# Negating the filter taps on GpSimd, and building the first spectrum before the second filter's rows

## The reference

```python
def bidir_long_conv(u, h_fwd, h_bwd, bias):
    filt = concat([h_fwd, zeros(1), h_bwd[1:][::-1]])
    spec = rfft(u, 2n) * rfft(filt, 2n)
    return irfft(spec)[:n] + u * bias
def hyena(u, lp):
    x1, x2, v = split(short_conv(u), 3)
    filt = hyena_filters(n, lp)        # a small MLP with sines, times exp(-t * decay)
    z = v
    for o, g in enumerate((x1, x2)):
        z = g * bidir_long_conv(z, filt[:, o, 0], filt[:, o, 1], bias[o])
    return z
def trunk_layer(x, mod, lp):
    shift, scale, gate = split(mod, 3)      # mod = silu(c) @ ada_w + ada_b
    h = rmsnorm(x) * (1 + scale) + shift
```

## Time and profile before

| what | value |
|---|---|
| median of 3 runs | 2737.1 us (2736.19 to 2737.31) |
| the profiled execution | 2737.1 us, span 2734.9 us |
| TensorE busy | 2426.1 us, 89% of the span |
| VectorE busy | 1319.2 us, 48% |
| ScalarE busy | 943.0 us, 34% |
| GpSimd busy | 172.8 us, 6% |
| mean granted clock of TensorE | 0.942 |

### The profile page before, as it was taken

One profiled execution on the slowest core, in us unless ns is written; L12 is line 12 of the kernel. 1 busy time (PEld: TensorE's weight loads), 2 busy tenths in 40 slices (PEclk: granted clock), 3 DMA queues, 4 the chain that ended last, 5 costly groups with the idle time before them and its releaser, 6 DMA issues. The chain is left out here.

```text
span 2734.9 us, 33688 instructions
## 1 busy us (share of the span) xinstructions
PE 2426.1 (89%) x13152; PEld 1596.1 (58%) x13152; DVE 1319.2 (48%) x2658; ACT 943.0 (34%) x1886; POOL 172.8 (6%) x184
## 2 busy tenths in 40 slices
PE   3999999899898987879859999999988989888798
PEld 1765765674476756554327567557745667565543
DVE  3352664564364474661133426545553644746611
ACT  2242113541253364651022421135412533646510
POOL 0120000001000000001202200010010000000012
PEclk8999999999999998989969999999999989989799
DMA  6430100100100000102155101000001000001021
GB/s 216 165 140 26 50 16 1 48 1 13 58 7 9 3 1 2 63 1 91 60 178 213 61 26 50 16 21 29 1 13 64 1 9 3 1 2 63 1 93 61
DMA packets 72136, 128.42 MB, mean 47 GB/s; under 512 B 22915, under 2 KB 36099, under 8 KB 70341
## 3 DMA queue, kind: packets, MB, share of 16 engines
q1 hardware_dynamic: 71864, 121.52, 13.0%
q10 hardware_dynamic: 112, 4.72, 0.5%
HBM read 109.02 MB, written 21.92 MB: 48 GB/s over the span
## 5 line engine op out<-in xcount | busy, mean ns | idle before, releaser
L609 PE MATMUL psum<-arena 128*32 128x256 f32 (+8 forms) x8496 | 1743.0, 451 | 123.8 <-DMA arena<-in_hy_decay 46.9
L609 PEld LDWEIGHTS psum<-arena 128*32 128x32 f32 (+3 forms) x8496 | 1013.1, 161 | 780.7 <-issue 526.3
L613 PE MATMUL psum<-ident,arena 128*128 128x128 f32 (+1 forms) x2248 | 366.6, 291 | 76.2 <-ACT arena L1284 30.0
L1763 DVE TENSOR_REDUCE st<-psum 128x1 f32<-128x1152 f32 (+1 forms) x288 | 352.0, 1235 | 137.1 <-PE psum L609 135.5
L1469 DVE TENSOR_TENSOR arena<-arena 128x64 f32<-128x64 f32 (+10 forms) x686 | 304.5, 490 | 175.8 <-ACT arena L1420 57.5
L613 PEld LDWEIGHTS psum<-ident,arena 128*128 128x128 f32 (+1 forms) x2248 | 268.1, 146 | 178.6 <-issue 59.7
L1268 ACT ACTIVATE arena<-psum,st 128x1152 f32<-128x1152 f32 (+1 forms) x288 | 324.8, 1129 | 118.8 <-DVE st L1763 115.3
L609 PE MATMUL psum<-k_parts,q_parts 96*128 96x384 f32 (+2 forms) x1000 | 300.4, 391 | 34.4 <-ACT arena L1268 22.9
L1284 ACT COPY arena<-psum 128x512 f32<-128x512 f32 (+1 forms) x344 | 170.6, 505 | 230.3 <-PE psum L613 229.2
L1469 DVE TENSOR_TENSOR arena<-psum,arena 128x512 f32<-128x512 f32 (+2 forms) x136 | 75.1, 553 | 355.6 <-PE psum L609 308.2
L609 PEld LDWEIGHTS psum<-k_parts,q_parts 96*128 96x128 f32 (+1 forms) x1000 | 181.5, 205 | 53.3 <-ACT arena L1268 36.6
(11 more groups left out here) (125 smaller groups left out, 1170.1 us busy)
## 6 DMA issues: line engine op xcount, KB each, us to landing
arena<-in_ada_w SPq DMA_DIRECT2D x12, 2048.0 KB, 9.0
arena<-in_w_in SPq DMA_DIRECT2D x10, 2048.0 KB, 9.0
arena<-out_xs SPq DMA_DIRECT2D x36, 512.0 KB, 4.7
out_xs<-arena SPq DMA_DIRECT2D x18, 512.0 KB, 2.6
arena<-in_w_out SPq DMA_DIRECT2D x4, 2048.0 KB, 7.9
out_xs<-in_x ACTq DMA_DIRECT2D x1, 4608.0 KB, 17.3
spectrum_kept<-arena SPq DMA_DIRECT2D x2, 2304.0 KB, 8.4
arena<-spectrum_kept SPq DMA_DIRECT2D x2, 2304.0 KB, 8.8
```

Source lines behind the costliest of these rows:

```text
L609: return nc.tensor.matmul(out, lhsT, rhs, start=start, stop=stop)
L613: return nc.tensor.transpose(out, src, ident[0:n, 0:n])
L1763: nc.vector.tensor_reduce(st[:, 16 + x % 4:17 + x % 4], psum[:, 512 * b0:512 * (b0 + nk)].rearrange("p (c n) -> p c n", c=nk)[:, :, 0:w], ...
```

## The change

It has four parts.

1. The copy of the tokens is started by SP, behind the six constants, and SP waits for it at the head of each layer, before the first parameter load. Before, ACT started it, and SP waited for it later.
2. The negation of the filter rows moves from ACT's list to GpSimd's: nine instructions of 128x256 in front of each butterfly, so 36 in the run.
3. On DVE the filter rows of o = 0 and the bias of slice 3 come behind the whole first spectrum.
4. On SP the store of the first spectrum comes ahead of the six token loads.

The numbers of lines shift a little: L1469 becomes L1463, L1597 L1586, L1608 and L1610 L1597 and L1599, L2016 L2007, and the negation is L2048.

```diff
--- before.py
+++ after.py
@@ -431,6 +431,7 @@
             sp.dma_start(craw[:, :, 1:2], I["c_ctx"].rearrange("(o k p) -> p k o", p=P, o=1)).then_inc(S.raw("constants"), 16)
             sp.dma_start(halves[:, :], I["halves"]).then_inc(S.raw("constants"), 16)
             sp.dma_start(negt[:, :], I["negt"]).then_inc(S.raw("constants"), 16)
+            sp.dma_start(xs[0], I["x"]).then_inc(S.raw("x_copied"), 16)
             with sp.Fori(0, DEPTH) as l:
                 def lay(name):
                     return I[name][bass.ds(l, 1)]
@@ -455,6 +456,7 @@
                     load(W[:, SLOT[c], :, 0:n], src.rearrange("o (k p) n -> p (o k) n", p=P),
                          f"weights{SLOT[c]}_loaded", c)
 
+                sp.wait_ge(S.raw("x_copied"), 16)
                 load(at(F_FEAT, TOK, parts=33), I["feats"], "filter_params")
                 load(at(A_FW, 64, parts=33), lay("hy_fw1").rearrange("o k n -> (o k) n"), "filter_params")
                 load(at(A_FW + 64, 64, parts=64), lay("hy_fw2").rearrange("o k n -> (o k) n"), "filter_params")
@@ -482,18 +484,17 @@
                 chunk()
                 chunk()
 
+                sp.wait_ge(*S.at("butterfly_pool", ("F", 1)))
+                sp.wait_ge(*S.at("spectrum1_made"))
+                sp.dma_start(spectrum_kept, at(HS, 4608)).then_inc(*S.up("spectrum1_kept", None, 16))
+
                 def load_x(t):
                     load(at(XN[t % RING], D), xs[bass.ds(l, 1)][:, rows(t), :].rearrange("o p n -> (o p) n"),
                          f"x{t % RING}_loaded", t)
 
-                sp.wait_ge(S.raw("x_copied"), 16)
                 sp.wait_ge(*K.emptied(("f3", 0, NT)))
                 for t in range(RING):
                     load_x(t)
-                sp.wait_ge(*S.at("butterfly_pool", ("F", 1)))
-                sp.wait_ge(*S.at("spectrum1_made"))
-                sp.dma_start(spectrum_kept, at(HS, 4608)).then_inc(*S.up("spectrum1_kept", None, 16))
-
                 chunk()
                 chunk()
 
@@ -1103,7 +1104,6 @@
                 act.wait_ge(*S.now("scalar_step"))
 
             act.wait_ge(S.raw("constants"), 16 * N_CONST)
-            act.dma_start(xs[0], I["x"]).then_inc(S.raw("x_copied"), 16)
             nc.scalar.activation(csil[:, :, :], craw[:, :, :], ACT.Tanh, scale=0.5).then_inc(S.raw("silu_ready"), 1)
             act.wait_ge(S.raw("ones_set"), 1)
             with act.Fori(0, DEPTH) as l:
@@ -1125,12 +1125,6 @@
                                          accum_out=st[:, t:t + 1]).then_inc(*S.up("x_squares", t))
 
                 for o in (1, 0):
-                    for t in range(TT):
-                        act.wait_ge(*K.emptied(("f3", o, t)))
-                        if t in (0, NT):
-                            act.wait_ge(*S.at("lag0_cleared", (o, t)))
-                        last = nc.scalar.mul(at(EO, TT, 3, GW)[:, t, 2, :], at(EO, TT, 3, GW)[:, t, 1, :], -1.0)
-                    last.then_inc(*S.up("filter_negated", o))
                     if o == 0:
 
                         act.wait_ge(*S.at("butterfly_sums", ("F", 1)))
@@ -1557,8 +1551,7 @@
 
                 add_ada_bias(0)
                 eo = at(EO, TT, 3, GW)
-                def filter_rows(o):
-
+                for o in (1, 0):
                     for t in range(TT):
                         job = ("f3", o, t)
                         v.wait_ge(*K.full(job))
@@ -1573,15 +1566,11 @@
 
                             v.wait_ge(*K.emptied(job))
                             nc.vector.memset(eo[0:1, t, 1, :], 0.0).then_inc(*S.up("lag0_cleared", (o, t)))
-
-                filter_rows(1)
-                add_ada_bias(1)
-                add_ada_bias(2)
-                add_ada_bias(3)
-                filter_rows(0)
-                add_ada_bias(4)
-                for o in (1, 0):
-                    if o == 0:
+                    if o:
+                        add_ada_bias(1)
+                        add_ada_bias(2)
+                    else:
+                        add_ada_bias(4)
                         modulation()
                         add_ada_bias(5)
                         gate_rows()
@@ -1609,6 +1598,8 @@
                                                    ALU.mult, ALU.add)
                     nc.vector.tensor_copy(at(HS + 4096 + GW, GW), at(B2 + 4096 + GW, GW)
                                           ).then_inc(*S.up(f"spectrum{o}_made"))
+                    if o:
+                        add_ada_bias(3)
 
                 xv = at(XV, TT, 768)
 
@@ -2048,7 +2039,14 @@
 
 
                 nc.gpsimd.memset(at(A_ADAB, 3072), 0.0).then_inc(*S.up("ada_bias_cleared"))
+                eo = at(EO, TT, 3, GW)
                 for o in (1, 0):
+                    for t in range(TT):
+                        pool.wait_ge(*K.emptied(("f3", o, t)))
+                        if t in (0, NT):
+                            pool.wait_ge(*S.at("lag0_cleared", (o, t)))
+                        last = nc.gpsimd.tensor_scalar(eo[:, t, 2, :], eo[:, t, 1, :], -1.0, None, ALU.mult)
+                    last.then_inc(*S.up("filter_negated", o))
                     if o == 0:
                         for t in range(RING):
                             inverse_root(("x", t), st[:, t:t + 1])
```

## The result

The changed kernel is slower. Its median is 2769.1 us (2765.09 to 2771.1, 4 runs) against 2737.2 us, a ratio of 1.0115 with a 95% interval of 1.0098 to 1.0133. The forecast was 2758.7 with a range of 2746 to 2771, so the measured time lies near its upper end. The profiled execution is a long one, 6.8 us over the median: 2775.9 us, span 2773.7, so 38.8 us over the span before.

A forecast was written before the change was run, and what follows sets the result against it. TensorE's own list was taken to bound the kernel. A 4.0 us later start plus 8.8 us in each of two layers added 21.6 us to 2737.1, giving 2758.7 us; range 2746 to 2771, its own working 2751 to 2764.

The forecast's parts named there:

- TensorE's list is the path, and nothing is made up later: From the forward transform of o = 1 to the token transposes, TensorE's own list sets the end; delays there stay.
- The spectrum's length and the wait: First spectrum ahead of bias 3: still 13.55 us, bank 4 free at 118.05, so TensorE stands still 5.4 us.
- the rival in which TensorE never runs out of banks: Rival, chance 0.10: VectorE finishes the spectrum before seven banks fill; no shift, 2741.1 us with the copy's 4.0 alone.
- The clock falls, and is back about when the columns begin: Behind TensorE's idle stretch: 1.2 GHz for filter tiles and `ada(4)`, full clock for the modulation columns; +8.8 us per layer.
- The transform then runs at full clock: Transform of o = 0 behind the columns: nothing added to the +8.8 us per layer for a slower clock.
- The rival with the late clock: Rival, chance 0.12: clock not back for the columns, which take twice as long; +13.9 us per layer, 2768.9 us.
- The copy: First layer's start: token copy on SP takes 15.3 us, parameters follow; TensorE starts at 30.4 us, +4.0 us once.
- The negation: Filter-row negations on GpSimd ahead of each butterfly: 0.5 us each, hidden behind TensorE's work, cost nothing.
- No slowing of the filter rows: VectorE's filter rows beside GpSimd's negations: no slowing taken; if each waited one out, +10.1 us instead of +8.8.
- The sum: Whole kernel: 4.0 + 2 x 8.8 = 21.6 us over the profiled 2737.1, so 2758.7 us, chance 0.50.

The follow-up runs named there:

- the order alone: Kernel before with only VectorE's order changed (bias 3 and filter rows of o = 0 behind the first spectrum): 2758.2 us, ratio 1.0063.
- the earlier bias 3: Changed kernel with bias 3 added inside the first butterfly, behind VectorE's first large instruction: 2749.5 us in one execution, then median 2764.5 us, ratio 1.0089 to the kernel before.
- the repeat: The changed kernel run once more as it is, with more rounds: 2768.8 us, ratio 1.0106 to the kernel before.
- the filled wait: Changed kernel with raw filter tiles 0 to 6 of o = 0 computed twice, to fill TensorE's wait: 2760.5 us, ratio 1.0085 to the kernel before.
- the run with ScalarE negating: Changed kernel with the negation left on ScalarE (copy, order and store changed): 2767.5 us, ratio 1.0101 to the kernel before.
- four slices ahead of the tiles: Kernel before with the copy started after the filter parameters landed, and `ada(0)` computed four times: 2711.2 us, ratio 0.9894 to the kernel before.

## Why the prediction came out as it did

*TensorE's list is the path, and nothing is made up later*: right. From the transposes on TensorE's idle time changed by little (131.3 to 129.8 us in the first layer, 120.8 to 120.4 in the second), and the order alone costs 19.3 us, where its profile lost 21.0 at the places.

*The spectrum's length and the wait*: right. 13.55 us predicted, 13.5 measured; a wait of 5.4 predicted, 5.2 measured, in both layers. The first butterfly kept its contention with GpSimd, so the rival in which TensorE never runs out of banks is out. That other banks follow behind bank 4 was shown by the earlier bias 3.

*The clock falls, and is back about when the columns begin*: right as far as it went. In the profiled execution it rose close to the end of `ada(4)`, and the columns began 8.9 us later than before, once the start is taken off; the transform started +9.2 against +8.8. In the repeat's second layer the clock was not back for the columns.

*The transform then runs at full clock*: this is the step that was mis-sized. It was put at nothing beyond the 8.8; the clock fell again, and the transform's part up to the gate rows took 25.9 and 25.3 us against 22.85 and 24.54, so 3.1 and 0.8 us more. With columns of 3.9 and 4.5 us instead of 3.6 the places lost 12.3 and 10.0 us in this execution, 11.0 and 12.7 in the repeat, against 8.8. The rival with the late clock (+13.9) had the right ingredients. Where columns and transform were both slow, in the repeat's second layer, it came near (12.7), elsewhere it was too high. The fall in the transform is not the change's alone: it is in the second layer of the kernel before, and the filled wait has it without an idle stretch. The part up to the gate rows took 25.3 to 25.9 us in all four profiled layers of the changed kernel. What sets the length of the fall, and whether the clock is back for the columns, is not settled; executions of one program differ in it.

*The copy*: 4.0 predicted, 4.8 measured in the changed kernel's profile, and from 4.0 to 5.2 in the profiles of the experiments with this part. It landed 16.8 us after its issue at 3.98 (15.3 taken), so it gained little from having the engines to itself, and the parameters then needed 10.5 us from their first issue at 20.76 (10.9 taken).

*The negation*: its price was too low, 0.82 to 0.85 us against 0.5, and its cost of nothing was right within the intervals, as the run with ScalarE negating shows. The last negation ends 2.6 us before the transform starts, so at an estimated 1.1 us apiece it would have begun to count. No slowing of the filter rows: right. Here the Trainium skill (SBUF — State Buffer, section Who interferes with whom) had said the same, that one SBUF input does not contend with GpSimd, and these rows with one operand from each memory now show it: 4.80 us for eight with either engine beside them.

*The sum*: 2758.7 against 2769.1. Of the 10.4 us missing, 0.8 is the copy and about 5 the clock at the places (12.3 + 10.0 - 17.6 = 4.7 in one execution, 6.1 in the other). The rest, some 4 us, is of the size by which executions differ in the unchanged stretches; the four runs of before, within 1.2 us of each other, had made this kernel look steadier than it is. That the measured time still lies inside the range, 1.9 us from its end, is owed to the late clock's rival, from which that end was taken; the working itself had reached to 2764.

## What to carry to other kernels

When an engine's work is put behind a long block, look for whose buffers it drains: TensorE could run only seven tiles ahead, and the block was 13.5 us long. When an operation moves to another engine, its place on that engine's list decides and not its own length: the same 36 negations cost nothing, or 19 us a layer, by where they stood (in a wait of TensorE, with VectorE's old order). And a transfer that is needed late should not be started ahead of small ones that are needed first: starting the copy only when the parameters had landed won 12 us.

## What the runs showed that was not expected

TensorE's clock can fall while it is never idle: in the filled wait it went to 0.50 in the columns at 129 us and stayed there for the first 5 us or so of the transform, and in the second layer of the kernel before it fell between 1473 and 1474. And nine filter tiles of 64 rows, back to back for 15.7 us, never brought it up, while it rose close to the end of the next slice of `ada` in both layers, behind it in the first and ahead of it in the second; four slices ahead of the tiles brought the transform forward by 7.1 and 8.7 us.

With one and the same program on one chip the kernel before spread by up to 16 us (2733.1 to 2749.3), and the changed kernel with the earlier bias 3 by 24. The profiled execution of the changed kernel missed its median by 6.8 us. A single time of 2749.5 stood for a median of 2764.5.

On GpSimd a multiplication of 128x256 by a constant took 0.82 us, more per element than its additions of two inputs (1.26 us at the least for 128x512).
